# Value products of the attention heads in column tiles of 32, and the next pair's scores ahead of the transposes

## The reference

```python
# 12 dilated heads in 3 groups (dilation 1, 4, 16), head width 64
scores = einsum('bgrnqd,bgrnkd->bgrnqk', qs, ks) * (hd ** -0.5)
scores = where(valid, scores, NEG_INF)
m = max(scores, axis=-1); p = exp(scores - m); den = sum(p, axis=-1)
o = einsum('bgrnqk,bgrnkd->bgrnqd', p, vs) / den[..., None]
# 8 neighbourhood heads: the same with a learned bias, 64 queries against 128 keys in each of 4 column blocks
yb = neighbourhood_attention(qb, kb, vb, rel_bias)
merged = gate_a * (ya @ w_branch_a) + gate_b * (yb @ w_branch_b)
return merged @ w_out
```

## Time and profile before

| | |
|---|---|
| median of three executions | 1158.97 us |
| the profiled execution's own time | 1158.87 us |
| its span, first to last instruction | 1157.1 us |
| TensorE busy | 1146.5 us, 99% |
| VectorE busy | 771.1 us, 67% |
| ScalarE busy | 584.5 us, 51% |
| chain of work that ended last | 96% TensorE, 1% issue, 1% VectorE |

### The profile page before, as it was taken

The page is one execution under the profiler, slowest core; times in us unless marked ns, Lnnn a source line. Parts: engine busy times, 40 slices in busy tenths (PEclk is TensorE's granted clock), DMA queues, the critical chain, the costliest instruction groups (busy, mean ns, idle before and its releaser), DMA issues.

```text
span 1157.1 us, 16180 instructions
## 1 busy us (share of the span) xinstructions
PE 1146.5 (99%) x6195; PEld 964.9 (83%) x6195; DVE 771.1 (67%) x997; ACT 584.5 (51%) x781; POOL 76.9 (7%) x116
## 2 busy tenths in 40 slices
PE   9999999999999999999999999999999999999997
PEld 6888888888878888888888888888887888888886
DVE  5866667756666676666686666677557577666665
ACT  6544446555554554444474444464555446544443
POOL 3622100000300000000000000000003000000000
PEclk9999999999999999999999999999999999999999
DMA  8866555653544565555546555556436536555551
GB/s 282 278 217 230 198 181 161 239 170 122 169 178 146 182 218 182 182 187 208 171 167 211 182 184 195 201 187 208 152 110 201 197 117 208 197 198 194 182 181 37
DMA packets 148242, 214.28 MB, mean 185 GB/s; under 512 B 9344, under 2 KB 114016, under 8 KB 147936
## 3 DMA queue, kind: packets, MB, share of 16 engines
q1 hardware_dynamic: 142960, 205.28, 52.3%
q0 software_dynamic: 4560, 6.97, 2.0%
q10 hardware_dynamic: 672, 1.37, 0.4%
HBM read 210.75 MB, written 5.12 MB: 187 GB/s over the span
## 4 chain that ended last, share of the span: by engine, by line
PE 96%; issue 1%; DVE 1%; DMA 0%; ACT 0%; ACTq 0%; POOLq 0%; POOL 0%; DVEq 0%
PE banks L1229 25%; PE banks L1163 16%; PE banks L1165 16%; PE banks L1164 16%; PE banks L1227 14%; PE banks L1226 4%; PE banks L1402 1%; PE banks L1201 1%; PE banks L1377 1%; PE banks L1363 1%; PE banks L1340 1%; DMA x<-x_dram 0%; PE banks L1352 0%; PE banks L1393 0%; PE banks L1424 0%
## 5 line engine op out<-in xcount | busy, mean ns | idle before, releaser
L835 DVE TENSOR_TENSOR w_lo<-raw,w_hi 128x2048 fp32r<-128x2048 f32 x190 | 435.5, 2293 | 187.2 <-ACT w_hi L599 187.2
L599 ACT ACTIVATE w_hi<-raw 128x2048 fp32r<-128x2048 f32 x190 | 363.6, 1915 | 230.5 <-PE banks L1165 228.2
L1229 PE MATMUL banks<-a_both,w_hi 128*128 128x512 f32 x1232 | 439.2, 396 | 0.0
L1227 PE MATMUL banks<-a_both,w_lo 128*128 128x256 f32 x1408 | 364.1, 279 | 0.0
L1227 PEld LDWEIGHTS banks<-a_both,w_lo 128*128 128x128 f32 x1408 | 265.4, 188 | 14.8
L1229 PEld LDWEIGHTS banks<-a_both,w_hi 128*128 128x128 f32 x1232 | 231.2, 188 | 47.2
L1163 PE MATMUL banks<-w_hi,a_both 128*128 128x512 f32 (+1 forms) x448 | 178.1, 398 | 0.0
L1165 PE MATMUL banks<-w_hi,a_both 128*128 128x512 f32 (+1 forms) x448 | 171.8, 383 | 0.0
L1164 PE MATMUL banks<-w_lo,a_both 128*128 128x512 f32 (+1 forms) x448 | 171.3, 382 | 0.0
L1163 PE MATMUL banks<-w_hi,hT_hi 128*128 128x512 f32 x320 | 125.0, 390 | 0.0
L1165 PE MATMUL banks<-w_hi,hT_lo 128*128 128x512 f32 x320 | 124.5, 389 | 0.0
(11 more groups left out here) (118 smaller groups left out, 957.7 us busy)
## 6 DMA issues: line engine op xcount, KB each, us to landing
raw<-ffn_w_up_dram SPq DMA_DIRECT2D x172, 512.0 KB, 4.2
raw<-w_in_dram SPq DMA_DIRECT2D x92, 512.0 KB, 4.4
raw<-ffn_w_down_dram SPq DMA_DIRECT2D x88, 512.0 KB, 3.9
raw<-w_out_dram SPq DMA_DIRECT2D x16, 512.0 KB, 4.1
raw<-w_branch_b_dram SPq DMA_DIRECT2D x8, 512.0 KB, 3.7
raw<-ffn_w_up_dram SPq DMA_DIRECT2D x8, 256.0 KB, 5.6
bias_rows<-bias_kinds POOLq DMA_DIRECT2D x32, 64.0 KB, 4.1
bias<-bias_rows SPq DMA_DIRECT2D x2, 1024.0 KB, 7.7
```

The costliest lines, as they stand in the source:

```text
L599: act.activation(w_hi[slot][:, :], raw[slot][:, :], ACT.Copy).then_inc(hi_done, 1)
L835: dve.tensor_tensor(w_lo[slot][:, :], raw[slot][:, :], w_hi[slot][:, :].bitcast(F32), ALU.subtract).then_inc(lo_done, 1)
L1227: mm = pe.matmul(pair[:, b, 0:SEQ], w_lo[slot][:, at:at + P], a_hi[:, k, :], start=False, stop=False)
L1229: mm = pe.matmul(pair[:, b, :], w, both, start=False, stop=k == KT - 1)
```

## The change

The value products are cut into pieces of 32 queries, each of which writes 32 of the 128 output partitions: 4 column tiles in rotation. The moving operand of each piece is the same 64 columns of values as before. The number of value matmuls in the program becomes four times as large for the dilated heads and twice as large for the neighbourhood heads. And in the burst after quarter (0,0) the scores of pair p now come before the transposes of pair p-1.

```diff
+QUARTER = P // 4
@@ times_v, neighbourhood heads
-                        mm = pe.matmul(bank[OB][b * NA_Q:(b + 1) * NA_Q, at:at + HD],
-                                       probsT[:, hh, 0, c * NA_Q:(c + 1) * NA_Q], v_near[:, c, d0:d0 + HD],
-                                       start=True, stop=True)
+                        for i in range(2):
+                            q0 = c * NA_Q + i * QUARTER
+                            part = slice(b * NA_Q + i * QUARTER, b * NA_Q + (i + 1) * QUARTER)
+                            mm = pe.matmul(bank[OB][part, at:at + HD], probsT[:, hh, 0, q0:q0 + QUARTER],
+                                           v_near[:, c, d0:d0 + HD], start=True, stop=True)
@@ times_v, dilated heads
                 for t in range(TT):
                     kts = range(TT) if keys(h) == SEQ else (t,)
+                    at = (hh * TT + t) * HD
                     for k in kts:
-                        at = (hh * TT + t) * HD
-                        mm = pe.matmul(bank[OB][:, at:at + HD], probsT[:, hh, k - kts[0], t * P:(t + 1) * P],
-                                       v[:, k, h * HD:(h + 1) * HD], start=k == kts[0], stop=k == kts[-1])
+                        for b in range(4):
+                            part = slice(b * QUARTER, (b + 1) * QUARTER)
+                            mm = pe.matmul(bank[OB][part, at:at + HD],
+                                           probsT[:, hh, k - kts[0], t * P + b * QUARTER:t * P + (b + 1) * QUARTER],
+                                           v[:, k, h * HD:(h + 1) * HD], start=k == kts[0], stop=k == kts[-1])
@@ mixer
                                 if (t, q) == (0, 0):
-                                    if before is not None:
-                                        turn_probs(l, 2 * before)
-                                        turn_probs(l, 2 * before + 1)
                                     if p is not None:
                                         pe.wait_ge(qkT_read, l * 10 + (2 * (p // 2) + 2 if p < DIL_PAIRS else 10))
                                         if p >= 1:
                                             pe.wait_ge(scores_read, l * HEADS + 2 * p)
                                         scores(l, p)
+                                    if before is not None:
+                                        turn_probs(l, 2 * before)
+                                        turn_probs(l, 2 * before + 1)
```

## The result

The changed kernel's median is 1152.72 us (1152.59 to 1152.99, four runs) against 1159.20 for the kernel before (1158.41 to 1160.61, four runs): ratio 0.9943, 95% interval 0.9929 to 0.9958, so 6.5 us faster. Two repeats (e6 and e10, on two different chips) gave 0.9955 (0.9942 to 0.9969) and 0.9949 (0.9935 to 0.9962), that is 5.3 and 5.6 us, with medians of 1154.17 and 1153.98.

A forecast was written before the change was run, and what follows sets the result against it. TensorE, busy 99% of the span, was taken as the bound. Value products -3.2 and the wait -0.65 made -3.8 us from 1158.87, so 1155.0, with the runs' median at 1155.1; range 1153.3 to 1160.9.

The forecast's parts named there:

- Value products: Value blocks in the mixer: four column tiles give 192 rounds of 55.6 ns, shorter blocks, 3.2 us less.
- The rival with 27 ns a matmul: Value blocks: spacing is per matmul, a round of four takes 107 ns, sum +6.0, 1165.0 us; chance 0.15.
- The wait for the exponentials: Step of pair 7, both layers: scores placed first cover TensorE's wait for ScalarE; 0.65 us less.
- The edges of the new order: Tiling changes around scores in 16 steps: cost assumed the same with a dense matmul on the other side; 0 taken.
- The bound of 1.6 us either way: Scores-and-transposes steps: one tiling edge of 0.1 us more or less in each of 16 steps.
- Later transposes cost nothing: Bursts: transposes 0.6 to 1.1 us later, covered by idle time, cost nothing; rival up to 5 us more, chance 0.05.
- The start: Program's first microseconds: no change forecast; the sum was taken from the profiled execution, 1158.87 us.
- the rounds: Value blocks: 192 rounds of four matmuls at 55.6 ns each; each ns a round moves the program 0.19 us.
- the sum of -3.8: Whole program: -3.2 from value products and -0.65 from the wait, giving 1155.1 us.

The follow-up runs named there:

- e6: Changed kernel measured again, nothing altered: 1154.17 us against 1159.47 for the kernel before.
- e10: Changed kernel measured a third time, nothing altered: 1153.98 us against 1159.54 for the kernel before.
- e3: Changed kernel with all value products in two column tiles of 64 queries instead of four of 32: 1155.27 us against 1159.38 for the kernel before.
- e5: Changed kernel with all value matmuls of one column tile before the next tile's: 1159.73 us against 1159.47 for the kernel before.
- e1: Kernel before with the 32-query column tiles alone, transposes still ahead of scores: 1155.44 us against 1159.38 for the kernel before.
- e2: Kernel before with the new order alone (scores ahead of transposes): 1157.99 us against 1159.38 for the kernel before.
- e8: Changed kernel with transposes of q and k directly behind the value products in four steps: 1154.13 us against 1159.54 for the kernel before.
- e11: Kernel before with 12 fulfilled waits at each of 160 places in TensorE's program: 1159.03 us against 1159.31 for the kernel before.
- e12: Changed kernel with the changes of e8 and e9 together: 1151.73 us against 1159.31 for the kernel before.
- e9: Changed kernel with scores of the pair after next directly behind the value products: 1152.01 us against 1159.54 for the kernel before.

## Why the prediction was wrong, step by step

- **Value products: right, in mechanism and size.** Forecast -3.2, measured -3.35. A round of 55.6 ns was taken and 56 measured; blocks of 1.25, 1.70 and 1.25 were forecast, and 1.24, 1.69 and 1.26 came. e3 and e5 support the reasons: the load of 128 columns paced the dilated products, the stream of 64 paces them now, and it takes overlapping tiles. The rival with 27 ns a matmul is refuted: 14 ns a matmul are kept up over 64 in a row, and within a round the starts lie 7 ns apart. The Trainium skill, "TensorE: Matmul & The Clock Gate", section "Wait — 56ns, not 53.3ns?", allows no two starts within 25 ns; these are in different tiles, and the measurement decides.
- **The wait for the exponentials: right.** Forecast -0.65, measured 0.37 and 0.39 in the two steps, of which 0.05 each belongs to the next point: -0.66. It would have grown without the new order (e1), so it was worth 0.9 here.
- **The edges of the new order: the step that failed.** It read "It costs the same if the dense matmul is on the other side of it, I assume", and "I take 0". Measured: 0.053 us less in each of 16 steps, 0.84 us. Behind a tiled block the first weight load starts together with its own matmul (316.00 in the changed kernel), where the next one starts 0.23 us ahead of its matmul (316.11 and 316.34): that first load is not covered. In the kernel before the block was followed by a dense matmul, whose first start comes 0.34 us before the second in place of 0.23 (as 316.00 and 316.34 above). In the new order a transpose follows; the two starts after the scores are 0.165 us apart where transposes follow each other by 0.108, so 0.057 is laid bare and not 0.107. A transpose's load is also the shorter one by line, 140 ns at the median in the changed kernel against 188 for line 1164, and these 48 ns are nearly all of the 0.05 us. e2 shows the gain alone, e8 shows it again in another place. The bound of 1.6 us either way held it; the value taken inside it, 0, was wrong.
- **Later transposes cost nothing: right.** No trace has a wait for `probsT`, and none a wait for `w_lo` in the mixer; the only one, 0.3 to 0.6 us in four traces (the changed kernel's first, e5, e11, e12), lies in the start.
- **The start: the other step that failed, and the larger term.** The sum read "From the profiled execution, 1158.87 (span 1157.1 and 1.8 around it), 1155.0": it took the first 15 us of that execution as given and put their change at nothing, without a reason. They were 1.4 us shorter in the changed kernel's profile. `x` was there 0.8 us earlier (second four transposes at 6.67 in place of 7.42). From there to the third four transposes it took 1.66 us in place of 2.97, the warm-up matmuls starting 0.22 us apart in place of 0.43: 1.3 more. Of this 0.7 went back to waiting for `w_lo`: the first dense matmul starts 0.73 us after the last warm-up matmul, in place of 0.03. This is what carried the first result out of the range: with the edge and the rounds alone the sum would have been about 1154.1, and both repeats are inside the range (1154.17, 1153.98).

So of the 2.7 us between the sum of -3.8 and the -6.5 measured, 0.8 is the edge, 0.2 the rounds, and the other 1.6 or so the start, 1.4 of it seen in the two profiles.

## To carry to other kernels

Where a matmul has few moving columns, look which of load and stream paces it, from loads and matmuls of two widths in the trace; if it is the load, cut the stationary side into column tiles until the load is shorter than the stream, and stop there (two tiles brought 2.7 of 3.35 us here). Pay for the edges of tiled blocks by the block: join tiled blocks with each other (0.19 us each here) and put a transpose, not a wide matmul, behind the last. And before a forecast of a few us, ask of the profile what varies from one execution to the next, or give the first transfers a range of their own.

## What was not expected of the hardware

- Tiles seem to be served past one another: with two matmuls in a row on each of four column tiles a block costs 0.83 us against 0.79 in rotation, with four in a row 2.54 against 1.23.
- Going from column tiles straight to row and column tiles (e9) costs 0.19 us less than two separate edges. The Trainium skill, "TensorEngine Tiling (Array Packing)", section "Key Properties", says that a change of tiling mode drains TensorE, and gives no price; here each separate block pays some 0.09 us on entry (0.32 after the last dense matmul in place of 0.23) and 0.11 on exit before a dense matmul.
- The same kernel's first 15 us vary by 2.7 us between profiles (14.54, 14.82, 17.24). They go with the landing of `x` and with whether TensorE's clock is at 2.4 GHz or still at 1.2 when the warm-up matmuls come, which the view of the granted clock shows only from the trace's first clock entry on; they lean with the length of TensorE's program.
